# Query squares in one ScalarE operation a tile, summed by groups on VectorE

## The reference, cut to what matters

```python
def rms_norm(t, g, eps=NORM_EPS):
    t32 = t.astype(jnp.float32)
    y = t32 * lax.rsqrt(jnp.mean(t32 * t32, axis=-1, keepdims=True) + eps)
    return (y * g.astype(jnp.float32)).astype(t.dtype)
...
q = apply_rope(rms_norm(q.reshape(B, Lp, N_HEADS, 2, HEAD_DIM), q_norm[l]), cos, sin)
k = apply_rope(rms_norm(k.reshape(B, Lp, N_HEADS, 2, HEAD_DIM), k_norm[l]), cos, sin)
```

## Time and profile before

| | |
|---|---|
| median of 3 runs | 1855.44 us (1855.35 to 1857.39) |
| the profiled execution's own time | 1858.07 us |
| its span in the trace | 1855.9 us |
| PE busy | 1827.1 us, 98% of the span |
| POOL busy | 1331.0 us, 72% |
| DVE busy | 1120.8 us, 60% |
| ACT busy | 582.7 us, 31% |
| granted TensorE clock | 0.9 or more of full speed in all 40 slices |

### The profile page before, as it was taken

One profiled execution on the slowest core, in us unless ns is written; L12 is line 12 of the kernel. 1 busy time (PEld: TensorE's weight loads), 2 busy tenths in 40 slices (PEclk: granted clock), 3 DMA queues, 4 the chain that ended last, 5 costly groups with the idle time before them and its releaser, 6 DMA issues.

```text
span 1855.9 us, 34398 instructions
## 1 busy us (share of the span) xinstructions
PE 1827.1 (98%) x12667; PEld 1643.5 (89%) x12667; DVE 1120.8 (60%) x1668; ACT 582.7 (31%) x1638; POOL 1331.0 (72%) x2400
## 2 busy tenths in 40 slices
PE   8999999999999999999999999999999999999999
PEld 8998888888999999999999998887768877888787
DVE  6998887877544333333468989888885433333233
ACT  4135566436332110101011246664362322010100
POOL 3767455446768888888898763446477799898985
PEclk9999999999999999999999999999999999999999
DMA  4221021112322222222232211111124222222232
GB/s 178 91 92 69 24 69 47 46 69 86 136 96 81 83 93 89 91 91 106 108 120 91 91 69 46 69 47 48 67 91 145 106 91 90 91 91 91 90 109 73
DMA packets 25549, 160.64 MB, mean 87 GB/s; under 512 B 3024, under 2 KB 3408, under 8 KB 7776
## 3 DMA queue, kind: packets, MB, share of 16 engines
q1 hardware_dynamic: 21888, 147.01, 22.3%
q10 hardware_dynamic: 3552, 12.15, 1.7%
HBM read 154.85 MB, written 4.29 MB: 86 GB/s over the span
## 4 chain that ended last, share of the span: by engine, by line
PE 85%; POOL 7%; DVE 3%; issue 3%; ACT 2%; DMA 0%; POOLq 0%; DVEq 0%; SPq 0%; ACTq 0%
PE psum L654 62%; PE psum L741 12%; POOL w_lo L544 4%; PE psum L806 2%; PE psum L838 2%; PE psum L755 2%; POOL w_lo L551 1%; PE psum L826 1%; ACT e L1056 1%; POOL w_hi L542 1%; PE psum L814 1%; PE psum L675 1%; PE psum L855 1%; PE psum L883 1%; DVE mx L1343 1%
## 5 line engine op out<-in xcount | busy, mean ns | idle before, releaser
L654 PE MATMUL psum<-u,w_hi 128*128 128x264 f32 (+1 forms) x4416 | 899.8, 315 | 9.9 <-POOL w_lo L544 5.6
L544 POOL TENSOR_TENSOR w_lo<-w_raw,w_hi 128x128 fp32r<-128x128 f32 x1504 | 759.8, 542 | 7.8
L654 PEld LDWEIGHTS psum<-u,w_hi 128*128 128x128 f32 x4416 | 666.3, 189 | 68.4 <-issue 9.0
L654 PE MATMUL psum<-u,w_lo 128*128 128x264 f32 (+1 forms) x2208 | 558.1, 313 | 0.0
L551 POOL TENSOR_TENSOR w_lo<-w_raw,w_hi 128x128 fp32r<-128x128 f32 x640 | 312.0, 526 | 118.7 <-ACT w_hi L1038 81.0
L654 PEld LDWEIGHTS psum<-u,w_lo 128*128 128x128 f32 x2208 | 362.3, 189 | 25.1
L496 DVE SCALAR_TENSOR_TENSOR psum<-xg,pvec,psum 128x512 f32<-128x512 f32 x440 | 300.9, 751 | 4.4 <-DVE xg L1483 2.2
L741 PE MATMUL psum<-w_hi,u 128*128 128x256 f32 x1536 | 286.3, 286 | 1.1 <-POOL w_lo L551 1.1
L741 PEld LDWEIGHTS psum<-w_hi,u 128*128 128x128 f32 x1536 | 236.3, 188 | 11.6 <-issue 10.0
L741 PE MATMUL psum<-w_lo,u 128*128 128x256 f32 x768 | 215.1, 280 | 0.0
L1648 DVE TENSOR_TENSOR relu<-relu 128x528 f32<-128x528 f32 (+1 forms) x64 | 66.3, 1036 | 234.7 <-ACT u L1238 119.5
(11 more groups left out here) (203 smaller groups left out, 2093.3 us busy)
## 6 DMA issues: line engine op xcount, KB each, us to landing
w_raw<-w_slabs SPq DMA_DIRECT2D x135, 1024.0 KB, 4.8
h<-x_t SPq DMA_DIRECT2D x4, 528.0 KB, 7.2
h<-x_t ACTq DMA_DIRECT2D x1, 2112.0 KB, 9.3
h_spill<-h ACTq DMA_DIRECT2D x8, 264.0 KB, 2.3
h<-h_spill ACTq DMA_DIRECT2D x1, 2112.0 KB, 10.3
out<-h SPq DMA_DIRECT2D x8, 256.0 KB, 2.0
r_b<-r_rows ACTq DMA_DIRECT2D x1, 1584.0 KB, 6.8
r_b<-r_rows ACTq DMA_DIRECT2D x1, 1536.0 KB, 7.4
```

The costliest lines, as they stand in the source:

```text
L544: last = nc.gpsimd.tensor_tensor(w_lo[:, b, c:c + P], w_raw[:, b, c:c + P], w_hi[:, b, c:c + P], ALU.subtract)
L654: last = nc.tensor.matmul(psum[:, 2 * slot + j, 0:n], w[:, b, cut], src[:, part, kc, at0:at0 + n], start=(kc == 0 and m == 0), stop=(kc == ...
```

## The change

For q tiles, the four squares of 64 columns with their sums become one square of 256 columns that writes into `rtmp`, and the four small ones of the meta tokens become one. VectorE then sums all tiles by groups of 64 in one operation (in the first layer with a second one for the meta tokens), at a new place `rs` in its order. GpSimd's `turn` of q overwrites `rtmp`, so it now also waits for that sum. k tiles stay as they are.

```diff
-VECTOR_ORDER = [{"zero": "35 rq 1",
-     "first": "... c0 k1 2 m10 rq 1 m11 5 m12 2 sub0 c1 7",
-     "mid": "... c0 m10 2 rq 1 m11 5 m12 2 c1 sub0 3",
+VECTOR_ORDER = [{"zero": "31 rs 4 rq 1",
+     "first": "... c0 k1 rs 2 m10 rq 1 m11 5 m12 2 sub0 c1 7",
+     "mid": "... c0 rs m10 2 rq 1 m11 5 m12 2 c1 sub0 3",
...
-    {"zero": "32 rq 2",
-     "first": "... c0 2 m10 6 m11 rq 1 m12 3 sub0 c1 5",
-     "mid": "... c0 1 m10 9 m11 5 m12 sub0 3 c1 rq 1",
+    {"zero": "28 rs 4 rq 2",
+     "first": "... c0 2 m10 2 rs 4 m11 rq 1 m12 3 sub0 c1 5",
+     "mid": "... c0 1 m10 5 rs 4 m11 5 m12 sub0 3 c1 rq 1",
...
@@ GpSimd, turn
+                if x == 0:
+                    pool.wait_ge(q_summed, layer * 4 + pair + 1)
@@ ScalarE, b_evict
+                    if what == "q":
+                        if t == 1:
+                            act.wait_ge(roped, (layer * 4 + pair) * 2)
+                        if meta:
+                            nc.scalar.activation(rtmp[0:META, 0, :], psum[0:META, bank, 2 * P:4 * P], ACT.Square)
+                        last = nc.scalar.activation(rtmp[0:tn, t, :], psum[0:tn, bank, 0:2 * P], ACT.Square)
+                    else:
...
                         for g in range(4):
                             last = nc.scalar.activation(squares[0:tn, g, :], psum[0:tn, bank, g * HD:(g + 1) * HD], ACT.Square, accum_out=ssq[0:tn, x, 4 * t + g:4 * t + g + 1])
@@ VectorE
+            def q_squares(layer, pair):
+                b_read_wait(dve, b_before(layer, pair) + b_of(layer, "q"))
+                dve.wait_ge(v_chain, chain.value())
+                part = lambda rows, t0, t1: V.tensor_reduce(ssq[rows, 0, 4 * t0:4 * t1], rtmp[rows, t0:t1, :].rearrange("p t (g d) -> p (t g) d", d=HD), AX_X, ALU.add)
+                if 0 in q_tiles(layer):
+                    chain.mark(part(slice(0, META), 0, 1))
+                announce(dve, part(slice(0, P), 1, NTOK), q_summed, layer * 4 + pair + 1)
```

More of the change, by code:

```diff
@@ L407, in build @@
         scaled = sem("scaled")
+        q_summed = sem("q_summed")
         qk_hi = sem("qk_hi")
@@ L1022, in b_evict @@
                     act.wait_ge(b_free[B_BANK[n - 1]], B_USES[n][B_BANK[n - 1]])
-                    if meta:
+                    if what == "q":
[5 more added lines that the diff above has]
+                    else:
+                        if meta:
+                            for g in range(4):
+                                nc.scalar.activation(meta_low[0:META, g * HD:(g + 1) * HD], psum[0:META, bank, 2 * P + g * HD:2 * P + (g + 1) * HD], ACT.Square, accum_out=ssq[0:META, x, g:g + 1])
                         for g in range(4):
-                            nc.scalar.activation(meta_low[0:META, g * HD:(g + 1) * HD], psum[0:META, bank, 2 * P + g * HD:2 * P + (g + 1) * HD], ACT.Square, accum_out=ssq[0:META, x, g:g + 1])
-                    for g in range(4):
-                        last = nc.scalar.activation(squares[0:tn, g, :], psum[0:tn, bank, g * HD:(g + 1) * HD], ACT.Square, accum_out=ssq[0:tn, x, 4 * t + g:4 * t + g + 1])
+                            last = nc.scalar.activation(squares[0:tn, g, :], psum[0:tn, bank, g * HD:(g + 1) * HD], ACT.Square, accum_out=ssq[0:tn, x, 4 * t + g:4 * t + g + 1])
                     last.then_inc(b_free[bank], 1)
@@ L1551, in _ @@
                             rope(layer, stage - 1, 1)
+                        elif name == "rs":
+                            q_squares(layer, stage)
                         elif name == "rq":
```

## The result

| | before | after |
|---|---|---|
| median of the runs on one chip (4 each) | 1855.39 us (1854.58 to 1857.39) | 1866.71 us (1866.24 to 1867.64) |
| profiled execution: time, span | 1858.07, 1855.9 us | 1867.64, 1865.9 us |
| ScalarE, VectorE busy | 583, 1121 us | 564.9, 1134.1 us |
| mean granted TensorE clock | 0.999 | 0.995 |

The ratio is 1.0062 (95% interval 1.005 to 1.0074): the change costs 11.3 us. 1864.6 was forecast, so the sign and the place hold, and the amount is 2.1 us too small. ScalarE lost the 18 us that it was to lose (19 forecast) and VectorE gained 13 (11 forecast).

The account below looks back on a forecast made before the run. TensorE, busy 1827.1 of 1855.9 us, was taken as the bound. Terms +4.8 (first layer), +4.4 (second) and +0.3 (other six pairs), less 0.3 for exponentials, gave +9.2 us and 1864.6 us, range 1857.8 to 1868.5.

Parts of the forecast that it names:

- Slack of the hand-over, 0.05 and 0.1 us: Stage 0, first and second layer: GpSimd finishes the v slab only 0.05 and about 0.1 us before TensorE starts it.
- `turn` at 142.8 and 4.7 us later: Stage 0: GpSimd's `turn` of q starts at 142.8 instead of 138.46 in the first layer, 4.7 us later in the second.
- The sum's price of 1.23, with meta 1.56: VectorE's sum over 1024 inputs takes 1.23 us; with the first layer's meta-token sum 1.56 us.
- The collision of `stats` with the low part, +0.6 and +0.9: Stage 0: VectorE's `stats` falls beside GpSimd's v-slab low part and delays it 0.6 and 0.9 us in the two layers.
- Given back, 0.1 and 1.2: TensorE's later wait for the q slab goes, returning 0.1 us in the first layer and 1.2 us in the second.
- The other six pairs, +0.3: Pairs after stage 0: later maxima on VectorE cost +0.3 us for all six, bounds 0 and +5.
- ScalarE's relief, 0: ScalarE's 19 us saving is worth 0 on the path, at most -3.7 us through TensorE's waits on exponentials.
- 0.9 or more of full speed throughout: Whole kernel: TensorE's granted clock stays at 0.9 or more of full speed, so nothing lets it go faster.
- the stalls are given back (1): Rival, stage 0 stalls: all but the sum's own price comes back, +1.8 us, 1857.2 us; chance 0.10.
- 2: Rival: ScalarE's relief decides and TensorE's nine waits at its scores go, -3.7 us, at most 1851.7 us; chance 0.05.
- 3: Rival, attention: maxima of six pairs come late and TensorE waits, +5 us on top, 1869.6 us; chance 0.09.
- the sum at half its price (4): Rival: VectorE's sum takes 0.6 us, -0.8 us in each layer, 1863.0 us; counted inside the forecast's 0.76 chance.

Follow-up runs that it names:

- Experiment 2: Kernel before with idle GpSimd products ahead of each layer's first `turn`: three gave 1868.70 us, ratio 1.0069; one gave 1857.67 us, ratio 1.0006.
- experiment 6: Changed kernel with stage 0's sum in front of the last eight VectorE taps instead of the last four: 1859.63 against 1855.74 us, ratio 1.0021.
- experiment 1: Change kept only in each layer's first pair: 1866.22 against 1856.80 us, ratio 1.0048; in all pairs but that one: 1855.57 us, ratio 0.9993.
- experiment 4: Kernel before with ScalarE's single square per q tile and no sums of q's squares: 1855.66 against 1855.74 us, ratio 1.0002.
- experiment 3: Changed kernel with stage 0's squares in their own buffer, `turn` not waiting, sum behind the rotary product: 1854.55 against 1855.74 us, ratio 0.9994.
- e_pair0_only: Kernel before with the change only in each layer's first pair (stage 0): 1866.22 against 1856.80 us, ratio 1.0048.
- e_sum_early: Changed kernel with stage 0's sum four VectorE taps earlier: 1859.63 against 1855.74 us, ratio 1.0021.
- e_low_first: Changed kernel, but in stage 0 GpSimd makes the v slab's low part before `turn` of q: 1858.96 against 1855.74 us, ratio 1.0019.
- e_sums_only: Kernel before plus VectorE's sums at the changed places, over constant data into an idle buffer, nobody waiting: 1858.46 against 1855.42 us, ratio 1.0016.
- e_pair0_old: Changed kernel with each layer's first pair as before, the other six pairs changed: 1855.57 us, ratio 0.9993.
- e_pool_late: Kernel before with one idle GpSimd product of 1.5 us ahead of each layer's first `turn`: 1857.67 us, ratio 1.0006.
- e_own_buffer: Changed kernel with stage 0's squares in their own buffer, so `turn` needn't wait for the sum: 1854.55 against 1855.74 us, ratio 0.9994.
- e_square_only: Kernel before with only ScalarE's single square per q tile, q's sums left out: 1855.66 against 1855.74 us, ratio 1.0002.
- e_pool_late3: Kernel before with three idle GpSimd products of 1.5 us each ahead of each layer's first `turn`: 1868.70 us, ratio 1.0069.

## Why the prediction was right, and where its sizes were off

**Slack of the hand-over, 0.05 and 0.1 us: right.** Experiment 2 moved only GpSimd and got the stalls.

**`turn` at 142.8 and 4.7 us later: right.** Measured 142.74, and 1084.18 on an axis 3.7 us later, that is 1080.5 against 1080.3. The reasoning from the queue of taps was tested by experiment 6.

**The sum's price of 1.23, with meta 1.56: right** (1.21 and 1.53), and so the square's (0.37 forecast, 0.39 measured).

**The collision of `stats` with the low part, +0.6 and +0.9: wrong.** The low part took 9.19 and 9.18 us instead of 9.34 and 9.23. The two do slow each other, but VectorE paid: `stats` took 3.8 us (152.11 to 155.94) instead of 2.35, its small operations took 0.38 or 0.39 us beside GpSimd's low part, and 0.20 behind its end at 154.97. No wait of TensorE in the changed kernel's profile goes back to `stats`. This is a term of 1.5 us that was not there.

**Given back, 0.1 and 1.2: right** (0.3 and 1.4). The wait at the first q slab went and came back at the scores (177.78, 0.92 us); in the second layer it really went. How much there is to give varies: that wait is 1.07 us in the first profile of before and 0.57 in the second.

**The other six pairs, +0.3: right within what can be told** (experiment 1: -1.2 us, interval -3.0 to +0.6; -0.4 by the rows).

**ScalarE's relief, 0: right** (experiment 4: -0.1 us, and experiment 3). What I took off for it, 0.3, is not there either.

**What no step of the sum held: the clock behind a stall.** "0.9 or more of full speed throughout" was read from slices of 46 us and taken for a state of the kernel, though the same trace shows about half speed behind the wait at 31.66. Behind the two stalls the half clock cost 1.6 and 2.0 us, and about 1.4 more at 1401 in the first profile of the change. The mechanism stood; a term was missing, and one was too large.

That the forecast came within 2.1 us is in part luck. Of its 9.2 us, 1.5 were a collision that cost TensorE nothing. Without it the same sum gives 1863.1 us, 3.6 too low. Put right in these terms, the others as forecast (no collision, 0.4 more given back, nothing taken off for ScalarE, 3.6 to 5.0 for the clock), it gives +11.2 to +12.6 against the medians' 11.3.

**The rivals.** That the stalls are given back (1) fell with the scores of the second layer, still 9.1 us late at 1119.26; 2 with experiments 3 and 4, 3 with experiment 1; the sum at half its price (4) with its 1.21 us.

**What stays open.** The half clock near 1391 to 1402 was there in both profiles of the change, in e_pair0_only, e_sum_early, e_low_first and e_sums_only, and not in the two of before, e_pair0_old, both e_pool_late, e_own_buffer and e_square_only. In all thirteen TensorE waits there for 1.8 to 1.9 us. I have no cause for which of them loses the clock. That it needs no change of the kernel is likely from the executions of the kernel before that were measured beside the experiments: the 11 with a mean clock of 1.000 have spans of 1850.6 to 1853.6 us, the 22 with 0.998 or 0.997 have 1854.2 to 1858.7. So this kernel too loses some clock in most executions, and its scatter goes with that; at which places isn't on record for those without a profile. The medians can't be divided between this and the rest.

## What to carry to other kernels

Before an operation moves from one engine to another, look at what that engine has queued at the moment when the operands are ready, and at the slack of the first hand-over behind it: here the sum cost 1.5 us and its place in the queue 3.5 us more (the squares were ready at 137.6), against a slack of 0.05. Price a stall of TensorE with the clock that comes back with it, from the granted clock behind stalls of that length in the same trace (here behind the wait at 31.66, in windows of a few microseconds and not in the profile page's slices) or in a small run with an added delay. When a wait exists only because a buffer is written anew, a buffer of its own takes it away, as experiment 3 did.

## What the runs showed of the hardware that I had not expected

**The clock after a stall.** The stalls of TensorE that the experiments made, and the granted clock behind them: 1.3, 1.5, 1.6 and 1.9 us, full; 2.0 and 2.6 us, about half; 4.4 to 4.7 us, about half in all eight cases (both layers of e_pool_late3, e_pair0_only and the two profiles of the change). The length alone does not fix it. The waits of 1.8 to 1.9 us near 1390 to 1400 had a fall behind them in six profiles and not in seven; the wait of 2.3 to 2.6 us near 29 to 31.5 us, which every kernel has, had one in ten and none in three (e_pair0_only, e_pair0_old, e_low_first); and in e_sums_only one came at 1197, behind a wait of only 1.00 us. Nor does the clock always fall at once: at 1401 it fell about 1.5 us after TensorE was back at work (1399.65). One such stretch cost 1.4 to 2.0 us of work. In the chain that ended last of the changed kernel, the low part and the 16 matmuls behind it:

```profile
150.83 4.15 POOL w_lo L552 x10
...
155.02 3.44 PE psum L758 x16
```

These 16 took 3.44 us, 0.215 each; the same product with the q slab starts every 0.11 us in the rows from 174.88 on.

**VectorE and GpSimd share something, and who pays is not fixed.** The same rotary product took 1.71 us beside GpSimd's low part in one execution of before, and 4.16 us in another; in the second case the sixteen GpSimd operations beside it took 6.69 us instead of 10.47. GpSimd's timeline in the first profile of before, and in the second:

```profile
352.81 6.69 POOL L551 TENSOR_TENSOR w_lo<-w_raw,w_hi 128x128 fp32r<-128x128 f32 x16
```

```profile
352.21 10.47 POOL L551 TENSOR_TENSOR w_lo<-w_raw,w_hi 128x128 fp32r<-128x128 f32 x16
```

The Trainium skill ("SBUF — State Buffer", section "SBUF: two separate sides") says that the one that starts first holds the shared port pair for its whole instruction and that the other is blocked. The rows agree that one of them pays almost all of the time, and that it can be either.
